# Token gates by slot on ScalarE, and gathers that add expert rows to the residual rows

## What is computed

```
# first block, end
h = rms_norm(x, norm2_g) * (1 + scale_f) + shift_f
group, two experts and two gates per token   # gates = softmax(top 2 logits) * group probability
order the 2048 (token, choice) pairs by expert, pad each expert to blocks of 128 slots
for each block:  out = (silu(xb @ w_gate[e]) * (xb @ w_up[e])) @ w_down[e]   # 1024 -> 512 -> 1024
y[token] += slot_gate * out[slot]            # two slots per token
x = x + gate_f * y
x = rms_norm(x, final_g)
# second block, begin
h = rms_norm(x, norm_mix) * (1 + sc_m) + sh_m
q, k, v, f = h @ fox_w_in ...                # 16 heads of 64, forgetting attention
```

## Time and profile before

| | |
|---|---|
| median of three runs | 2546.28 us |
| the profiled execution's own time | 2546.85 us |
| its span, first to last instruction | 2545.2 us |
| TensorE busy | 2350.4 us, 92% |
| VectorE busy | 1946.7 us, 76% |
| ScalarE busy | 1349.8 us, 53% |
| GpSimd busy | 650.7 us, 26% |
| mean granted TensorE clock | 0.962 |
| DMA | 535.85 MB, mean 211 GB/s |

### The profile page before, as it was taken

One profiled execution on the slowest core, in us unless ns is written; L12 is line 12 of the kernel. 1 busy time (PEld: TensorE's weight loads), 2 busy tenths in 40 slices (PEclk: granted clock), 3 DMA queues, 4 the chain that ended last, 5 costly groups with the idle time before them and its releaser, 6 DMA issues. The chain is left out here.

```text
span 2545.2 us, 33466 instructions
## 1 busy us (share of the span) xinstructions
PE 2350.4 (92%) x11726; PEld 1976.5 (78%) x11726; DVE 1946.7 (76%) x2466; ACT 1349.8 (53%) x1908; POOL 650.7 (26%) x523
## 2 busy tenths in 40 slices
PE   5898979869999999999489999999899999999999
PEld 3676668757788878887379999998688888878887
DVE  5888368669989899888688888887867666656786
ACT  2242333247777777776477677676524443443432
POOL 1005544224333333333631011111024233310000
PEclk8998989879999999999699999999899999999999
DMA  6678456489968799998631111111431434487774
GB/s 256 178 234 259 159 174 224 157 310 376 362 251 334 276 387 403 392 403 335 224 109 42 50 51 50 50 39 45 180 116 68 164 145 163 157 318 282 280 266 149
DMA packets 181170, 535.85 MB, mean 211 GB/s; under 512 B 17439, under 2 KB 77443, under 8 KB 167737
## 3 DMA queue, kind: packets, MB, share of 16 engines
q1 hardware_dynamic: 163756, 470.71, 51.1%
q0 software_dynamic: 12592, 45.63, 4.7%
q10 hardware_dynamic: 4700, 17.92, 1.8%
HBM read 443.90 MB, written 90.33 MB: 210 GB/s over the span
## 5 line engine op out<-in xcount | busy, mean ns | idle before, releaser
L1644 PE MATMUL psum<-w_high,block_hT_high 128*128 128x512 f32 x576 | 234.2, 407 | 19.7 <-DVE w_low L1281 16.3
L1281 DVE TENSOR_TENSOR w_low<-w_up,w_high 128x2048 fp32r<-128x2048 f32 x72 | 190.8, 2689 | 54.1 <-ACT w_high L1275 54.1
L1646 PE MATMUL psum<-w_high,block_hT_low 128*128 128x512 f32 x576 | 226.8, 394 | 0.0
L1645 PE MATMUL psum<-w_low,block_hT_high 128*128 128x512 f32 x576 | 226.6, 393 | 0.0
L1644 PE MATMUL psum<-w_qkv_high,fox_hT_high 128*128 128x384 f32 (+1 forms) x512 | 184.3, 360 | 16.6 <-issue 8.5
L1275 ACT ACTIVATE w_high<-w_gate 128x2048 fp32r<-128x2048 f32 x74 | 141.2, 1912 | 92.3 <-DMA w_gate<-in_w_expert_gate 86.5
L1379 POOL TENSOR_TENSOR block_out<-block_out,late_rows 128x1024 f32<-128x1024 f32 x35 | 98.1, 2803 | 356.0 <-ACT block_out L1533 356.0
L1644 PE MATMUL psum<-mix_hT_high,w_in_high 128*128 128x512 f32 x400 | 167.2, 418 | 21.9 <-DVE w_in_low L729 15.8
L1281 DVE TENSOR_TENSOR w_low<-w_gate,w_high 128x2048 fp32r<-128x2048 f32 x74 | 171.1, 2315 | 19.9 <-ACT w_high L1275 19.7
L1644 PE MATMUL psum<-w_mlp_out_high,hidden_part_high 128*128 128x512 f32 x448 | 174.6, 390 | 1.9 <-DVE hidden L3871 1.8
L1645 PE MATMUL psum<-w_qkv_low,fox_hT_high 128*128 128x384 f32 (+1 forms) x512 | 176.2, 344 | 0.0
(11 more groups left out here) (496 smaller groups left out, 6723.1 us busy)
## 6 DMA issues: line engine op xcount, KB each, us to landing
w_gate<-in_w_expert_gate SPq DMA_DIRECT2D x32, 2048.0 KB
w_up<-in_w_expert_up SPq DMA_DIRECT2D x32, 2048.0 KB, 10.5
w_down<-in_w_expert_down SPq DMA_DIRECT2D x31, 2048.0 KB, 10.6
w_mlp_out_quarters<-in_w_mlp_out SPq DMA_DIRECT2D x78, 512.0 KB, 6.9
hidden_part<-hidden_parts SPq DMA_DIRECT2D x54, 512.0 KB, 4.4
v_aug<-in_w_ada SPq DMA_DIRECT2D x48, 512.0 KB, 4.5
expert_rows<-block_out POOLq DMA_DIRECT2D x34, 512.0 KB
v_aug<-in_ada_w SPq DMA_DIRECT2D x32, 512.0 KB, 4.5
```

What stands on the lines that cost most here:

```text
L1281: dve.tensor_tensor(wl[:, par, half], raw[kind][:, half], wh[:, par, half].bitcast(F32), ALU.subtract).then_inc(s_wl, 1)
L1644: pe.matmul(out, sh, mh, start=start, stop=False)
L1645: pe.matmul(out, sh, ml, start=False, stop=False)
L1646: return pe.matmul(out, sl, mh, start=False, stop=stop)
```

## The change

It has three parts. (a) In `moe`, the gates are brought from token order to slot order by one-hot matmuls as the slots were: two new VectorE products (`gob`), 16 matmuls of 96 columns, and one VectorE reduction give `gsl`[position, block]. GpSimd copies a block's column into `gcol` two blocks ahead. ScalarE applies it as its scale when it copies the down product from PSUM; VectorE does so for the last block. (b) In the join, the gathers write with an add straight into the residual rows `xr`, one after the other for each tile, so `first_result` and `second_result` go. (c) The buffers freed give five of `xr` and four of `zr`, and the lists of SP, GpSimd, ScalarE and VectorE are put in a new order.

```diff
+            gob = sbuf(c2, "block_gates", [P, 2, TT, 2, MAXB], F32R)      # and gth, gtl, gsl, gcol
...
+                    def gate_column(n, u, left):
+                        if left >= 2:
+                            pool.tensor_copy(gcol[:, u:u + 1], gsl[:, bass.ds(n + 2, 1)]).then_inc(s_gc, 1)
...
                     def step(n, u, left):
                         gather(n, u, left)
                         evacuate(n, u, left)
+                        gate_column(n, u, left)
...
                     turn(1)
+                    pe.wait_ge(t_gob, 2)
+                    for k in range(2):
+                        for t in range(TT):
+                            ins = pe.matmul(bank[7][:, 0:2 * MAXB], ohp[:, k, t, :], gob[:, k, t].rearrange("p h m -> p (h m)"), start=k + t == 0, stop=k + t == TT)
+                    ins.then_inc(t_gmm, 1)
                     pe.wait_ge(s_gg, 1)
                     turn_gated()
...
-                            act.activation(ob[:, u, 0:HALF], bank[5], ACT.Copy)
-                            act.activation(ob[:, u, HALF:D], bank[6], ACT.Copy).then_inc(s_ob, 1)
+                            act.wait_ge(s_gc, n + 1)
+                            act.activation(ob[:, u, 0:HALF], bank[5], ACT.Copy, scale=gcol[:, u:u + 1])
+                            act.activation(ob[:, u, HALF:D], bank[6], ACT.Copy, scale=gcol[:, u:u + 1]).then_inc(s_ob, 1)
...
+                    dve.tensor_copy(gth[:], gate2[:].rearrange("p t k -> p k t")).then_inc(t_gth, 1)
+                    dve.wait_ge(t_gth, 1)
+                    dve.tensor_tensor(gtl[:], gate2[:].rearrange("p t k -> p k t"), gth[:].bitcast(F32), ALU.subtract).then_inc(t_gth, 1)
...
                     gated(0, 1)
+                    dve.wait_ge(t_gth, 2)
+                    dve.tensor_tensor(gob[:, :, :, 0, :], ohb[:], over(gth[:].bitcast(F32), MAXB), ALU.mult).then_inc(t_gob, 1)
+                    dve.tensor_tensor(gob[:, :, :, 1, :], ohb[:], over(gtl[:], MAXB), ALU.mult).then_inc(t_gob, 1)
                     low_h(1)
-                    split_low(dve, "gate", 2, 0)
+                    split_low(dve, "gate", 2, 0, (0,))
+                    dve.wait_ge(t_gmm, 1)
+                    dve.tensor_reduce(gsl[:], bank[7][:, 0:2 * MAXB].rearrange("p (h m) -> p m h", h=2), X, ALU.add).then_inc(t_gsl, 1)
+                    split_low(dve, "gate", 2, 0, (1,))
...
-                    for k in range(2):
-                        sp.wait_ge(s_g[k][0], 16)
                     residual(2)
+                    residual(3)
+                    sp.wait_ge(s_g[0], 16)
                     weights(1)
+                    residual(4)
...
+                    def gather(t, k):
+                        if k == 0 and t >= 2:
+                            pool.wait_ge(s_x1[t % 5], 16 if t < 7 else 32)
+                        if k == 1:
+                            pool.wait_ge(s_g[t], 16)
+                        pool.indirect_dma_start(xr[t % 5], None, moe_dram,
+                                                bass.IndirectOffsetOnAxis(ap=rows_i[:, k, t:t + 1], axis=0), compute_op=ALU.add).then_inc(s_g[t], 16)
...
-                    def first_result(t):
...
-                    def second_result(t):
...
                     def final_scaled(t):
-                        if t >= 2:
-                            dve.wait_ge(s_xs[t % 2], 16 * (t // 2))
-                        dve.wait_ge(s_x2, t + 1)
-                        dve.tensor_tensor(zr[:, t % 2, :], xr[t % 3], final, ALU.mult).then_inc(s_z, 1)
+                        if t >= 4:
+                            dve.wait_ge(s_xs[t % 4], 16)
+                        dve.wait_ge(s_g[t], 32)
+                        dve.tensor_tensor(zr[:, t % 4, :], xr[t % 5], final, ALU.mult).then_inc(s_z, 1)
```

More of the change, by code:

```diff
@@ L1233, in moe @@
             s_om = sem("b_out_scaled")
+            s_gc = sem("b_gate_column")
+            t_gth, t_gob, t_gmm, t_gsl = [sem("t_" + n) for n in ("gates_split", "gates_by_block", "gates_summed", "slot_gates")]
             grow = late[:, 0:D]
@@ L1403, in _ @@
                     pool.tensor_tensor(late[:, 2 * D:3 * D], late[:, 2 * D:3 * D], late[:, 4 * D:5 * D], ALU.add).then_inc(t_fg, 1)
+                    pool.wait_ge(t_gsl, 1)
+                    for u in range(2):
+                        pool.tensor_copy(gcol[:, u:u + 1], gsl[:, u:u + 1]).then_inc(s_gc, 1)
                     n_pairs = over_blocks(pool, step)
@@ L1689, in attention @@
             with ExitStack() as early:
-                r0 = sbuf(early, "result0", [P, 2, D])
-                r1 = sbuf(early, "result1", [P, 2, D])
-                zr = sbuf(early, "final_rows", [P, 2, D])
+                x4th = sbuf(early, "fourth_rows", [P, D])
+                x5th = sbuf(early, "fifth_rows", [P, D])
+                zr = sbuf(early, "final_rows", [P, 4, D])
                 x3rd = sbuf(early, "third_rows", [P, D])
@@ L1701, in attention @@
             final, fgain, fshift = [late[:, n * D:(n + 1) * D] for n in range(1, 4)]
-            xr = (late[:, 4 * D:5 * D], late[:, 5 * D:6 * D], x3rd[:])
-            s_mg, s_x2, s_z, s_sq1, s_sq2, s_v1, s_v2, s_rt = [sem("j_" + n) for n in
-                ("first_result", "second_residual", "final_scaled", "square", "squares", "eps", "second_eps", "rstd")]
+            xr = (late[:, 4 * D:5 * D], late[:, 5 * D:6 * D], x3rd[:], x4th[:], x5th[:])
+            s_z, s_sq1, s_sq2, s_v1, s_v2, s_rt = [sem("j_" + n) for n in
+                ("final_scaled", "square", "squares", "eps", "second_eps", "rstd")]
             s_xn, s_sh, s_tr, s_hh, s_hl, s_xo, s_kz = [sem("j_" + n) for n in ("normed", "shifted", "turned", "high", "low", "out", "zeroed")]
-            s_g = [[sem(f"j_gather{k}{u}") for u in range(2)] for k in range(2)]
-            s_x1 = [sem(f"j_x1_{u}") for u in range(3)]
-            s_xs = [sem("j_store0"), sem("j_store1")]
+            s_g = [sem(f"j_added{t}") for t in range(TT)]
+            s_x1 = [sem(f"j_x1_{u}") for u in range(5)]
+            s_xs = [sem(f"j_store{u}") for u in range(4)]
             s_wf, s_wfh, s_wfl, s_lz, s_ft, s_fx, s_fa, s_fe, s_fl, s_fm, s_fs, s_fst = [sem("v_" + n) for n in
@@ L1801, in _ @@
                     store(0)
-                    residual(3)
+                    residual(5)
                     store(1)
+                    residual(6)
                     weights(2)
-                    residual(4)
-                    residual(5)
                     store(2)
-                    store(3)
-                    residual(6)
-                    store(4)
                     residual(7)
-                    store(5)
-                    store(6)
+                    for t in range(3, 7):
+                        store(t)
                     forget_half(0)
```

130 lines of the change are left out of this document (57 added, 73 removed).

## The result

The changed kernel takes 2562.93 us (median of five executions, 2554.91 to 2571.07) against 2547.55 for the kernel before (five executions): ratio 1.0067 [1.0045, 1.0088]. The same kernel measured again, as e12, gave 1.0070 [1.0044, 1.0096]. Both together, weighted by their intervals: 1.0068 [1.0052, 1.0085], some 17 us. The forecast was -5.6 us with a range up to 2556. The profiled execution of the changed kernel is its fastest of the five, 2554.91 us with a span of 2553.3, so its trace shows 8 of the 17 us.

The account below looks back on a forecast made before the run. It took the join to be bound by latencies, no engine full, with seven landings in a row deciding. Loop 0, preamble 0, last block +0.05 and join -5.6 us gave 2541.25 us (median 2540.7), range 2531 to 2556.

Parts of the forecast that it names:

- What bounds the join, and the form of the sum: Join: no engine is full, so latencies bound it; landings and GpSimd's list sum to the last turn, -5.6 us.
- the seven landings: Join: seven gather landings in a row on GpSimd's list decide when the last turn comes; 6.75 us each.
- the formula: Join: the last turn comes at 1243.9 us plus seven times a gather's time from issue to landing.
- rival 3: Join: GpSimd's gains are given back elsewhere, as by a list waiting for a late tile; -3 to +3 us, chance 0.15.
- The size of L: Join: an adding gather's time from issue to landing is 6.75 us: plain 5.2 plus one more transfer, 1.57.
- break-even: Join: the landing time, 7.55 us, above which the stage turns slower than before, by 7 us per us.
- Rival 2: Join: adding gathers are slow and transfers queue, landings 8.7 us and over; +10 us at 9; chance 0.2.
- Rival 1: Join: adding is free, landings near 5.2 to 6 us; -11 to -16 us, so 2533; chance 0.25.
- I take 0: Preamble and expert loop: the gates by slot cost nothing; preamble ends -2 and +1.3 us, loop 0.
- Cover at the start: Start of join: first turn 4 to 5 us later, but first projection only 1 to 2 later, at some 1243.
- GpSimd beside VectorE: Join: with fewer VectorE operations some GpSimd ones fall from 1.2 to 0.2 us; -1.4 us possible, left in the range.

Follow-up runs that it names:

- e12: The changed kernel as it is, measured again in five rounds against the kernel before: ratio 1.0070.
- e3: The kernel before with only the changed kernel's new join, its expert phase kept and no gates applied: ratio 1.0043 to the kernel before, 2558.84 us.
- e5: The changed kernel with SP's weight, forget-weight and later residual loads held until both gathers of tile 0 have landed: ratio 1.0067 to the kernel before.
- e8: The changed kernel with the two weight loads that fall in the join bringing only a quarter of their rows: ratio 1.0053 to the kernel before.
- e1_copy: The changed kernel with all 16 gathers of the join copying instead of adding, waits and order kept: ratio 0.9986 to the kernel before, 2545.35 us.
- e13: The kernel before with gates by slot alone, but no gate applied in ScalarE's copies or the last block's product: ratio 1.0025 to the kernel before.
- e9: The changed kernel with, from tile 3 on, a tile's first adding gather issued only when the tile before is whole: ratio 1.0141 to the kernel before.
- e7: The kernel before with 12 of its 16 gathers adding onto what their buffers hold, nothing else changed: ratio 1.0027.

## Why the prediction was wrong

**What bounds the join, and the form of the sum: right for the seven landings, short at the end.** The seven landings of its chain measured 7.5, 9.6, 8.5, 10.3, 7.35, 6.9 and 7.0, sum 57.2, mean 8.2. With 2.0 us for the later start the formula gives 1243.9 + 57.2 + 2.0 = 1303.1; 1307.07 was measured. The 4 us left over lie at the end. Between the landings the terms came out 1.2 us shorter than I had them, though an adding gather's issue takes 1.54 to 2.66 us. But from tile 7 whole to the last turn I had 6.65 us (product and square, rstd, scaled and shifted) and it was 11.9: VectorE's list keeps tile 6 waiting for tile 7's landing, and TensorE then turns tile 7 only behind tile 6's products. (It was 11.3 to 11.9 in e3, e5, e8 and e12 too.) The trace of before could have told me: there it is 9.5 us, from the end of the second add, 1287.26, to 1296.77.

```profile
1285.99 1.27 DVE L2566 SCALAR_TENSOR_TENSOR late_rows<-result,token_gates,late_rows 128x1024 f32<-128x1024 f32 x1
```

This is the place that rival 3 named. No run here changes that order.

**"The size of L": the step that failed.** I took 6.75 us, of plain 5.2 plus one more transfer of 1.57; over the seven landings the runs showed 8.2, which is 9.9 us of the join. With the 4.0 us at the end it turns the forecast -5.6 into the measured +8.3. For an adding gather alone I was near: 7.0. The error is that I priced L with nothing beside it, while the sum puts two adding gathers in flight in its middle and loads at its start. What I had in hand was the earlier trace rows and the busy share of 61%; I used them for the second rival (doubled gathers make 90% of DMA, L over 8.7) and gave that 0.2. Measured: 85%, mean L 8.2, break-even 7.55. "Collectives: The Full Stack", part 3, of the Trainium skill says, in its section on the fold count, that a reducing DMA is half as fast, as it reads two sources through one ring. It says so of collectives; the queue's 1.88 here agrees with the factor. That the cause is the two sources no run here shows.

**Rival 2, the mechanism that won:** its place holds (second gathers released by landings) and so does its reason (DMA share 85%, where it had 90%). At the measured L of 8.2 its price of 7 us per us of L gives +4.3; that the join came to +8.3, near the +10 it had at L = 9, is in part the end of the join. **Rival 1** can be read from e1_copy: with adding free, and part (a) in it, the time would be -3.6 us (0.14% of 2546, interval -0.31 to +0.02%), not -11 to -16. Two terms that I had left out show in its trace: the 4.8 us for the squares ahead of rstd(3), and 10.3 us instead of 6.65 from tile 7 taken up (1282.75) to the last turn (1293.08).

**"I take 0" for part (a): wrong by some 6 us, outside its ends of -2 and +1.3,** though the steps that I priced cost nothing. From the last turn of gathered rows to the first gate product there were 6.28 us before (548.93 to 555.21) and are 6.29 now (552.73 to 559.02), with the new work in it:

```profile
548.93 1.04 PE L1417 MATMUL psum<-ident,gathered 128*128 128x128 f32 x8
...
552.73 1.04 PE L1432 MATMUL psum<-ident,gathered 128*128 128x128 f32 x8
555.48 1.99 PE L1478 MATMUL psum<-block_gates,position_onehot 128*128 128x96 f32 x16 [1.70 <-DVE block_gates L1638]
557.31 1.02 PE L1446 MATMUL psum<-ident,gated 128*128 128x128 f32 x4
559.02 0.80 PE L1675 MATMUL psum<-w_high,block_hT_high 128*128 128x512 f32 x1 [0.69 <-DVE w_low L1288]
```

The 2 us that a faster clock might have given did not come: from the first product on, they took some 0.63 us each, not 0.4, for 3.5 us before the change (to 558.73) and for 5.3 us after it (to 564.30); over all traces it is 3.5 to 4.8 us without part (a) and 3.5 to 5.3 with it. The copies in the loop cost 0.69 us each, 0.60 without a scale; e13 shows no gain from taking the scale out.

```profile
L1553 ACT ACTIVATE block_out<-psum,block_gate_column 128x512 f32<-128x512 f32 x34 | 23.4, 689 | 72.1 <-PE psum L1677 72.1
```

**Cover at the start:** tile 0 was to be whole 13.5 us after the first gather; it took 17.1 (7.5 + 9.6). First turn 9.2 us later where 4 to 5 were forecast, first projection at 1248.84 where 1243 was. The forecast that VectorE would no longer be late there held: the projection began 3.76 us after TensorE's last work, on the split of its tile. **VectorE** 39.6 us in the window where 46 were forecast: less of the work lies in the window. From the first gather to the last turn it is 63.6 us before and 45.2 now, so the forecast held. **GpSimd beside VectorE:** its small operations did fall, most to 0.19 us, which agrees with the section "Who interferes with whom" of "SBUF — State Buffer" in the Trainium skill. It bought little: most were covered, and rstd(0) took 2.4 us (1238.09 to 1240.47) where 2.9 were counted and 1.5 hoped for. **Part (c):** SP's early loads cost 2.4 us on tile 0's two landings (e5), where 1.5 was allowed, but issuing them later gave nothing: e5's time is the changed kernel's, and its join 2.7 us longer, which one pair of traces can't tell.

**The account in time.** Part (a) +0.23%, part (b) with (c) +0.43% (e3), together 0.66% against 0.68% measured. Within (b) and (c), in traced join time: order and lifted VectorE work -5.9 us (e1), adding +14.2. Of the 14.2, 1.5 lie behind the taking up of tile 7 (11.9 against 10.3).

## What to carry to other kernels

An adding DMA was not a free add here: it held the DMA engines nearly twice as long for the same bytes, and two that must follow each other put two landings on the path where there was one. It did not pay in a stage of latencies where VectorE, busy 79%, was not the bound; whether it pays where VectorE is the bound and the DMA engines have room, no run here shows. The order of a list needs the same care: here an operation of the last tile, ahead of the tile before it on VectorE, held both. And price a landing with what will be in flight beside it: the busy share after the change, worked out first, says which landing time to use.

## What the runs showed of the hardware

- An adding gather of 128 rows of 4 KB: 7.0 us to landing with no other gather in flight (e9), 4.7 to 5.0 plain (e1); 8.5 to 10.3 beside others; issue on GpSimd at least 1.54 us against 0.93.
- The gathers' queue held the engines 1.88 times as long for the same 8.39 MB, and nearly in proportion for 8 or 12 of 16 (27.0 and 30.2%).
- An issue on SP took longer beside adding gathers: the load of 0.1 KB took 8.91 us to issue (8.78 in e12, 5.36 in e3, 6.80 in e7), and 2.83 before and 3.27 in e1, with plain gathers. In e5, where it is issued behind tile 0's landings, it took 2.30.

```profile
1229.60 8.91 SPq L1829 DMA_DIRECT2D forget_bias<-in_fox_b_f  x1
```

- Part (a), of which the traces show no step on the path, still measured +0.23% [0.10, 0.36] over two sets of runs.
